# Four weight units instead of two share the arriving chunks behind three normalised residuals

## What is computed

```python
def first_block(x, ...):
    h = swiglu(rms_norm(x, ff1_norm_pre), ff1_w_gate, ff1_w_up, ff1_w_down)
    x = x + 0.5 * rms_norm(h, ff1_norm_post)
    h = hybrid_mixer(rms_norm(x, mix_norm_pre), w_in, ..., w_out, lambda_init)
    x = x + rms_norm(h, mix_norm_post)
    h = swiglu(rms_norm(x, ff2_norm_pre), ff2_w_gate, ff2_w_up, ff2_w_down)
    return x + 0.5 * rms_norm(h, ff2_norm_post)

def second_block(x, mem, ...):          # two layers, A then B
    for i in range(2):
        h = rmsnorm(x, mix_norm[i])
        x = x + mixer_i(h, mem) @ w_o[i]
        x = x + swiglu_2(rmsnorm(x, ffn_norm[i]), w_gate[i], w_up[i], w_down[i])
    return rmsnorm(x, final_norm)
```

## Time and profile before

| what | us |
|---|---|
| median of 3 runs | 2499.93 |
| lowest, highest of the runs | 2479.05, 2517.47 |
| profiled execution, its own time | 2520.88 |
| its span, first to last instruction | 2519.1 |
| TensorE matmul (PE) busy | 2404.0, 95% of the span |
| GpSimd (POOL) busy | 990.4, 39% |
| VectorE (DVE) busy | 950.6, 38% |
| ScalarE (ACT) busy | 842.6, 33% |

### The profile page before, as it was taken

The page is one execution under the profiler, slowest core; times in us unless marked ns, Lnnn a source line. Parts: engine busy times, 40 slices in busy tenths (PEclk is TensorE's granted clock), DMA queues, the critical chain, the costliest instruction groups (busy, mean ns, idle before and its releaser), DMA issues.

```text
span 2519.1 us, 28094 instructions
## 1 busy us (share of the span) xinstructions
PE 2404.0 (95%) x10238; PEld 1834.3 (73%) x10238; DVE 950.6 (38%) x1420; ACT 842.6 (33%) x1403; POOL 990.4 (39%) x444
## 2 busy tenths in 40 slices
PE   7999998999999899999899999999998889999997
PEld 6888886874444678888677588888786546888886
DVE  4111346358534341124475141123522651411245
ACT  5222234325533232222332242222333652422222
POOL 4544444550000364444453144444344322444442
PEclk9999999999956899999999799999999778999999
DMA  5222221330000122222122022222222001222221
GB/s 206 100 100 88 95 100 67 119 127 23 1 1 1 50 100 96 88 99 100 67 101 84 34 100 100 87 96 100 84 101 84 1 1 50 100 98 87 99 100 67
DMA packets 29223, 201.60 MB, mean 80 GB/s; under 512 B 3296, under 2 KB 3936, under 8 KB 5472
## 3 DMA queue, kind: packets, MB, share of 16 engines
q1 hardware_dynamic: 28512, 199.60, 22.5%
q10 hardware_dynamic: 640, 1.05, 0.2%
HBM read 197.49 MB, written 2.10 MB: 79 GB/s over the span
## 4 chain that ended last, share of the span: by engine, by line
PE 89%; DVE 4%; ACT 3%; POOL 2%; issue 1%; DMA 0%; DVEq 0%; ACTq 0%; SPq 0%; POOLq 0%
PE PS L796 25%; PE PS L798 25%; PE PS L797 25%; PE PS L1052 4%; PE PS L990 4%; PE PS L1024 2%; POOL X L402 1%; DVE ACC L1210 1%; PE PS L1152 1%; PE PS L1140 1%; PE PS L833 1%; DVE XL L1202 1%; DVE NMAX L1391 1%; PE PS L897 0%; PE PS L995 0%
## 5 line engine op out<-in xcount | busy, mean ns | idle before, releaser
L380 POOL TENSOR_TENSOR WL<-RAW,WH 128x1024 fp32r<-128x1024 f32 x368 | 910.4, 2478 | 1392.6 <-ACT WH L435 1392.6
L796 PE MATMUL PS<-XH,WH 128*128 128x512 f32 (+1 forms) x2168 | 853.5, 394 | 31.6 <-DVE XL L1202 31.5
L797 PE MATMUL PS<-XL,WH 128*128 128x512 f32 (+1 forms) x2168 | 842.8, 389 | 0.0
L798 PE MATMUL PS<-XH,WL 128*128 128x512 f32 (+1 forms) x2168 | 842.4, 389 | 0.0
L435 ACT ACTIVATE WH<-RAW 128x1024 fp32r<-128x1024 f32 x368 | 388.6, 1060 | 1300.2 <-PE PS L798 1262.6
L796 PEld LDWEIGHTS PS<-XH,WH 128*128 128x128 f32 x2168 | 412.0, 190 | 128.6 <-issue 41.0
L797 PEld LDWEIGHTS PS<-XL,WH 128*128 128x128 f32 x2168 | 412.1, 190 | 85.6 <-issue 3.8
L798 PEld LDWEIGHTS PS<-XH,WL 128*128 128x128 f32 x2168 | 411.6, 190 | 83.6
L1253 DVE TENSOR_TENSOR HL<-WORK,HH 128x512 fp32r<-128x512 f32 x80 | 186.0, 2326 | 257.1 <-ACT HH L548 208.7
L796 PE MATMUL PS<-HH,WH 128*128 128x512 f32 x704 | 274.2, 390 | 6.3 <-DVE HL L1253 6.3
L798 PE MATMUL PS<-HH,WL 128*128 128x512 f32 x704 | 273.9, 389 | 0.0
(11 more groups left out here) (174 smaller groups left out, 1761.2 us busy)
## 6 DMA issues: line engine op xcount, KB each, us to landing
RAW<-wstream SPq DMA_DIRECT2D x183, 1024.0 KB, 4.8
X<-xT SPq DMA_DIRECT2D x1, 2048.0 KB, 16.2
outT<-WORK SPq DMA_DIRECT2D x8, 256.0 KB, 2.2
RAW<-wstream SPq DMA_DIRECT2D x2, 512.0 KB, 6.4
WORK<-memT SPq DMA_DIRECT2D x1, 1024.0 KB, 7.5
PB<-WORK ACTq DMA_DIRECT2D x8, 127.8 KB, 2.4
CST<-consts SPq DMA_DIRECT2D x1, 912.0 KB, 11.3
WORK<-constsb SPq DMA_DIRECT2D x1, 256.0 KB, 12.1
```

The lines of the kernel that those rows point to most:

```text
L380: pool.tensor_tensor(WL[:, s, :, :].rearrange("p a b -> p (a b)"), RAW[:, s, :], WH[:, s, :, :].rearrange("p a b -> p (a b)").bitcast(F), ...
L796: pe.matmul(o, wh, xh, start=start, stop=False)
L797: pe.matmul(o, wh, xl, start=False, stop=False)
L798: return pe.matmul(o, wl, xh, start=False, stop=stop)
```

## The change

Three entries of `SIDE` go from 2 to 4. A new function `wavefront` on PE takes the four units: for every chunk the units 0, 1 and 2 in turn, with the fourth joining after the second chunk (it takes chunks 0 and 1 there, and then each chunk behind unit 2). `ssq` stands inside it, after unit 0's last chunk, ahead of the last chunk of units 1, 2 and 3. In `project` the flips of units that finish in it are held back until unit 4 has been issued. POOL, ACT, DVE and the DMA queue keep their programs. The whole difference:

```diff
--- before.py
+++ after.py
@@ -188,7 +188,7 @@
 HID_TURN = [("kw", 0), ("nq", 2)]
 POOL_X_AT = 2
 EARLY = 6
-SIDE = {"mem": 1, "ff1": 1, "proj1": 2, "ff2": 2, "projA": 2, "ffnA": 2, "kv": 2, "ffnB": 2}
+SIDE = {"mem": 1, "ff1": 1, "proj1": 4, "ff2": 4, "projA": 4, "ffnA": 2, "kv": 2, "ffnB": 2}
 SSQ_AT = {"mem": 2, "ff1": 2, "proj1": 3, "ff2": 3, "projA": 3, "ffnA": 3, "kv": 3, "ffnB": 3}
 LAG_T = 4
 LAG_V = 6
@@ -822,6 +822,25 @@
                         if k == KC - 1:
                             mm.then_inc(unit_done, 1)
 
+            def wavefront(units, stage, norm):
+
+                for u, bank in units:
+                    have(u)
+                steps = [(k, j) for k in range(KC) for j in range(3)]
+                steps[6:6] = [(0, 3), (1, 3)]
+                for k in range(2, KC):
+                    steps.insert(steps.index((k, 2)) + 1, (k, 3))
+                for n, (k, j) in enumerate(steps):
+                    u, bank = units[j]
+                    if j == 0:
+                        pe.wait_ge(xn_ready, KC * XN[stage] + k + 1)
+                    mm = three(PS[:, bank, :], WH[:, u % RING, k, :], WL[:, u % RING, k, :],
+                               *split_x(stage, k), k == 0, k == KC - 1)
+                    if k == KC - 1:
+                        mm.then_inc(unit_done, 1)
+                        if j == 0:
+                            ssq(norm, 7)
+
             def ssq(name, bank, cols=S):
 
                 if name.startswith("sub"):
@@ -835,13 +854,14 @@
             def gate_up(l, stage):
                 u0 = U0[f"gu{l}"]
                 n = SIDE[stage]
-                side_by_side([(u0 + j, j) for j in range(n)], stage)
+                if n == 4:
+                    wavefront([(u0 + j, j) for j in range(n)], stage, PRE[l])
+                else:
+                    side_by_side([(u0 + j, j) for j in range(n)], stage)
                 for j in range(n, 4):
                     if j == SSQ_AT[stage]:
                         ssq(PRE[l], 7)
                     features(u0 + j, j, stage)
-                if SSQ_AT[stage] == 4:
-                    ssq(PRE[l], 7)
                 with pe.Fori(0, FC // 2 - 1) as i:
                     for f in range(2):
                         pe.wait_ge(gu_free, i * 2 + (FC * l + f + 1))
@@ -931,7 +951,10 @@
             def project(part, stage, norm=None, cols=S):
                 jobs = JOBS[part]
                 side = SIDE.get(stage, 1) if norm else 1
-                if side > 1:
+                late = []
+                if side == 4:
+                    wavefront([(x["u"], x["n"]) for x in jobs[:side]], stage, norm)
+                elif side > 1:
                     side_by_side([(x["u"], x["n"]) for x in jobs[:side]], stage, cols)
                 for i, x in enumerate(jobs):
                     if side > 1 and i < side:
@@ -945,7 +968,7 @@
                             pe.wait_ge(taken, x["t"] - 3)
                         features(x["u"], x["t"] % 4 if part == "projB" else x["n"] % 4, stage, cols=cols,
                                  first=x["n"] == 0)
-                    if i == SSQ_AT.get(stage, 1) - 1 and norm:
+                    if i == SSQ_AT.get(stage, 1) - 1 and norm and side < 4:
                         if part == "mem":
                             pe.wait_ge(consts_in, 32)
                         ssq(norm, 7, cols)
@@ -953,7 +976,11 @@
                             pe.wait_ge(lam_prod, 1)
                             pe.matmul(PS[:, 6, 0:2], ONES, LAM[:, 0:2], start=True, stop=True).then_inc(lam_sum, 1)
                     if i >= 1 and "f" in jobs[i - 1]:
-                        flip(jobs[i - 1])
+                        late.append(jobs[i - 1])
+                    if side < 4 or i >= 4:
+                        for y in late:
+                            flip(y)
+                        late = []
                     if (x["kind"], x["j"]) in HID_TURN:
                         hidden_turned(HID_TURN.index((x["kind"], x["j"])))
                 if "f" in jobs[-1]:
```

## The result

The changed kernel took 2554.73 us in the median of 4 runs (2532.84 to 2582.67), against 2500.09 before: 54.6 us more, a ratio of 1.0204 with a 95% interval of 1.0135 to 1.0274. Timed again more often it had 2553.57 us and a ratio of 1.0184 (1.0115 to 1.0253). The ratios leave out executions in a slower state of the chip, as the one of 2582.67, so they are not the quotients of the medians; they stand for 51 and 46 us. Both intervals hold 1.02, so the runs do not tell on which side of 2% the change lies.

The account below looks back on a forecast made before the run. The prediction took PE to bound the kernel, busy 2404.0 of 2519.1 us. Its terms, 47.35 - 1.1 + 5.8 = +52 us, were added to the median 2499.93 for 2552, range 2532 to 2570.

Parts of the forecast that it names:

- The start: At each stage PE's first matmul waits for unit 3's low part from POOL; first stage 434.6 instead of 419.43.
- 87 matmuls and a restart: From PE's start to `ssq`: 19.72 us at full clock plus 1.94 for the low clock; `ssq` about 15.8 later per stage.
- Behind `ssq`: Unit 4 starts about 6.05 us after `ssq` instead of 6.42, with PE waiting some 3.2; -1.1 us over three stages.
- The clock in the new gap: In PE's 3.2 us wait ahead of unit 4 the clock falls, costing 1.94 us per stage, +5.8 in all.
- What follows: Behind each stage the ring of weights keeps up and no later slack takes the loss back; cost 0.
- the units are not late: Rival: low parts of units 2 and 3 are there at 419.4; at most +2.2 us a stage, 2506; chance 0.07.
- The clock holds: Rival: no fall of the clock in the wait ahead of unit 4; +46.2 us, 2546; chance 0.20.
- Long restarts: Rival: each of six restarts costs the first stage's 2.98 us; +58, 2558; chance 0.18 shared with the dry ring.
- The ring runs dry: Rival: PE waits for weights of units 5 to 8; 8.4 us more, 2560; chance 0.18 shared with long restarts.
- without the traffic between POOL and DVE: Side estimate at each stage: without shared-port contention PE would start 0.85 us sooner and the sum be 2.5 smaller.
- the 1 us for the squares and as much for chunks: All that better sharing could win at a stage: about 1 us of waits for squares and as much for chunks.

Follow-up runs that it names:

- e8_lazy_waits: The changed kernel with each unit's wait at that unit's first matmul, POOL's order unchanged; stages of 44.7, 45.9 and 44.7 us.
- e2_pool4: The changed kernel with POOL_X_AT = 4, so POOL makes units 2 and 3's low parts ahead of the residual additions; stages 38.9, 35.4, 39.2 us.
- e3_pool4_refill: e2_pool4 with ACT also rounding units 2 and 3 ahead of the branch's rstd in the down stages; stages of 36.1, 35.4 and 36.1 us.
- e4_early_unit4: e3_pool4_refill with ACT also rounding unit 4 ahead of the pre-norm's rstd; stages of 34.0, 33.6 and 34.0 us, ratio 1.0012.
- e7_after_early4: The changed kernel with one edit, ACT rounding unit 4 ahead of the pre-norm's rstd; stages of 47.4, 48.0 and 47.5 us.

## Why the prediction was right

The forecast was 2552 and the result 2554.73. Its own steps:

1. *The start.* Forecast 434.6 instead of 419.43, thus 21.7 us into the stage; at the second stage 895.30, which is 22.6 into it. Measured 21.66, 21.65, 21.69. The second stage came 1.0 sooner than forecast, which is the 0.9 by which this start varies: in the repetition it was 22.6.
2. *87 matmuls and a restart.* Forecast 19.72 + 1.94 = 21.66 from the start to `ssq`; measured 21.80, 22.16, 21.96. The restart cost 2.1 to 2.4, a little above the mean of the three before. `ssq` came 15.84, 15.30 and 16.03 us later than in the profile of before, 47.2 together against a forecast of 47.35. That this agrees so closely is luck: 1.0 too much at the second start and 0.9 too little for the restarts cancel.
3. *Behind `ssq`.* Forecast 6.05 to unit 4 and a wait of 3.2; measured 5.94, 5.83, 5.93 with waits of 2.83, 2.73, 2.82. The term was -1.1 and came out at -2.0 (45.2 less 47.2), of which 0.4 is the first stage's flip, which only moved and is paid behind unit 4.
4. *The clock in the new gap.* I took a fall at each stage, 3 x 1.94 = 5.8. It fell at all three, but cost 1.6 each, 4.8. This term is the one that was mis-sized. Without it the sum would have been 46, 8.4 below the measured difference and below the 2% line. That it fell at all three was partly luck: the forecast chose between two rows of other places, and at the second stage of e8_lazy_waits the same gap of 2.73 was followed by no fall.
5. *What follows.* Forecast 0. From the second stage's `ssq` to the next branch's it was 347.9 us before and 349.1 after, the fall included.

The sum of the measured terms is 50.0, against 52 forecast and 54.6 measured by the medians, or 51 and 46 by the two ratios; these differences are within the intervals and show in no stage. So the mechanism is shown, and that 2552 met 2554.73 within 3 us is luck.

Of the rivals, *the units are not late* was shown false by the change, and its price was shown right by e2_pool4: with the low parts there, the second stage lost 0.5 us, and 1.6 for the fall behind unit 4, 2.1 where I had at most 2.2. *The clock holds* was false. *Long restarts* was false, since none cost over 2.5 in the change. *The ring runs dry* was false: besides the six waits named above the list has only the one of 0.5 us, which stands at 16.3 us, ahead of all three stages.

One step was too small without harm to the forecast. I wrote that without the traffic between POOL and DVE PE would start 0.85 sooner. That looked at POOL's side alone. On DVE's side the same meeting delayed the squares by 3.6 us, more than the 1 us for the squares and as much for chunks that I had given to better sharing.

## What to carry to other kernels

A wait on a counting semaphore is a wait for everything that the other engine has queued ahead of that count; before a wait is moved up, read the other engine's program order and the time of that row in the trace. Before more work is brought in to cover a gap, look how large the gap is: here about 2 us a stage, while the squares and not the chunks ended it. And where a stretch that nobody changed differs by 30 us between two executions, compare the touched stages, each from a fixed point, and not the spans.

## What the runs showed of the hardware that I had not expected

**The clock fell after PE had resumed.** Behind the gap of 2.8 us the first one to three matmuls still ran at the full rate. The changed kernel, first and second stage:

```profile
465.80:468.60 2.80, 0.03 (x1) 0.00 (x0) 1.84 (x4) 1.22 (x2) 2.44 (x2) 1.00 0.26 61
468.60:470.00 1.40, 1.34 (x4) 1.14 (x5) 0.00 (x0) 0.00 (x0) 1.40 (x1) 0.66 0.89 206
470.00:472.00 2.00, 2.00 (x6) 1.52 (x6) 0.00 (x0) 0.20 (x1) 0.84 (x1) 0.50 0.87 200
909.00:912.00 3.00, 0.27 (x2) 0.08 (x1) 1.40 (x3) 2.97 (x4) 2.35 (x1) 1.00 0.00 0
912.00:914.00 2.00, 2.00 (x7) 1.58 (x8) 1.70 (x3) 1.89 (x3) 1.59 (x1) 0.70 0.39 70
```

The granted clock is 1.00 through the gap and falls to 0.50 (1.2 GHz) about 0.4 and 0.9 us after PE is busy again, for some 3.3 us. The last `ssq` of the kernel before, on which the forecast rested, reads the same way; its clock fell near 2507.7, just behind its start:

```profile
2507.59 1.97 PE L833 MATMUL PS<-ACC,CST 128*128 128x512 f32 x2 [3.22 <-DVE ACC L1210]
```

I first took the second and third stage for unharmed, because their first matmul behind the gap was quick. In the profiles of the change, its repetition, e2_pool4, e3_pool4_refill and e8_lazy_waits 14 of 15 such gaps were followed by a fall, worth 1.6 us each (the exception is the second stage of e8_lazy_waits); in e4_early_unit4 and e7_after_early4, where the gap at this place was 0.8 to 1.0 us, there was none in 6.

**Two instructions on DVE pay for the subtractions on POOL.** A DVE instruction with two SBUF inputs grew from 0.75 to 2.57 us and another from 0.69 to 2.88 while POOL made low parts, and the low parts from 2.4 to 2.8. The Trainium skill, "SBUF — State Buffer", "SBUF: two separate sides", has the loser block until the other is through. The trace agrees: in the kernel before POOL's two low parts end at 428.85 + 2.85 = 431.70 and at 434.50, and the two DVE instructions 0.6 us behind them, at 432.25 and 435.05. What it cost was not the 0.4 us on POOL but the 3.6 us on the chain of squares.

**The attention stretch varied most.** It took 397 to 450 us in kernels whose programs are the same there, with a granted clock between 0.67 and 0.91 over the window from 600 to 850 us. What sets it from run to run was not tried.
